# Expert weights of a mixture-of-experts layer loaded in rows of 4 KB, with the down product in parts by whole rows

## The reference

```python
def hier_moe(x, rg, rg_b, re, re_b, wg, wu, wd):     # x: 256 tokens x 1024, 16 experts
    ...                                              # top-1 group of 4, top-2 experts in it
    out = jnp.zeros(t.shape, jnp.float32)
    for e in range(N_EXPERTS):
        h = jax.nn.silu(t @ wg[e]) * (t @ wu[e])     # wg, wu: 1024 x 512, float32
        out = out + combine[:, e:e + 1] * (h @ wd[e])   # wd: 512 x 1024, float32
    return out
...
h = layer_norm(DEEPNORM_ALPHA * h + moe, ln2_g[l], ln2_b[l])
```

## Time and profile before

| | |
|---|---|
| Median of three runs | 524.52 us (523.69 to 528.94) |
| Profiled execution, its span | 522.5 us |
| Between that span and the median | 2.0 us |
| Busy: TensorE matmul, VectorE, ScalarE, GpSimd | 92%, 55%, 28%, 32% of the span |
| The eight expert passes | 275.3 to 509.8 us of the span |

### The profile page before, as it was taken

One profiled execution on the slowest core, in us unless ns is written; L12 is line 12 of the kernel. 1 busy time (PEld: TensorE's weight loads), 2 busy tenths in 40 slices (PEclk: granted clock), 3 DMA queues, 4 the chain that ended last, 5 costly groups with the idle time before them and its releaser, 6 DMA issues.

```text
span 522.5 us, 6332 instructions
## 1 busy us (share of the span) xinstructions
PE 478.6 (92%) x2478; PEld 300.7 (58%) x2478; DVE 287.3 (55%) x497; ACT 148.2 (28%) x223; POOL 165.2 (32%) x94
## 2 busy tenths in 40 slices
PE   7799999997979868769789999999999999999990
PEld 7689998875757756647673434344443434344440
DVE  6069968999999987983552321414031321414136
ACT  3075455554175285322311010101010010101010
POOL 8927707198583909743330000000000000000002
PEclk9999999998999998999999999999999999999996
DMA  7990455545551657459955999999999999999932
GB/s 267 261 355 3 160 182 182 181 161 189 182 174 44 219 211 290 162 170 369 382 205 188 389 386 387 386 387 384 386 387 387 387 387 387 386 387 387 386 133 81
DMA packets 76984, 142.92 MB, mean 274 GB/s; under 512 B 6776, under 2 KB 11009, under 8 KB 76960
## 3 DMA queue, kind: packets, MB, share of 16 engines
q1 hardware_dynamic: 75728, 140.29, 74.8%
q10 hardware_dynamic: 752, 2.11, 1.0%
q0 software_dynamic: 480, 0.20, 0.3%
HBM read 141.54 MB, written 1.05 MB: 273 GB/s over the span
## 4 chain that ended last, share of the span: by engine, by line
PE 61%; DVE 31%; DMA 3%; ACT 2%; issue 2%; SPq 0%; ACTq 0%; DVEq 0%
PE bank L1269 21%; PE bank L1294 11%; DVE ring L1505 7%; PE bank L1235 6%; PE bank L1308 5%; DVE rounded L1426 4%; DVE work L1606 4%; PE bank L1166 4%; PE bank L922 3%; PE bank L951 3%; DMA ring<-in_w_in_dram 3%; DVE ring L1603 2%; DVE ln1p L1463 2%; DVE rounded L1554 2%; PE bank L964 1%
## 5 line engine op out<-in xcount | busy, mean ns | idle before, releaser
L1269 PE MATMUL bank<-ring,gates 128*64 128x512 f32 x512 | 111.6, 594 | 0.4 <-ACT gates L864 0.4
L1040 PE MATMUL bank<-rounded 128*128 128x512 f32 x384 | 94.4, 401 | 6.5 <-POOL rounded L578 4.7
L1040 PEld LDWEIGHTS bank<-rounded 128*128 128x128 f32 x384 | 71.6, 191 | 25.5 <-POOL rounded L578 5.0
L613 POOL TENSOR_TENSOR work<-work,lnp 128x512 f32<-128x512 f32 x1 | 1.3, 1319 | 248.6 <-ACT work L877 248.6
L1269 PEld LDWEIGHTS bank<-ring,gates 128*64 128x64 f32 x512 | 36.2, 137 | 74.3 <-issue 74.3
L1759 DVE TENSOR_TENSOR gates<-gates,bank 128x512 f32<-128x512 f32 x8 | 5.5, 688 | 96.5 <-PE bank L1269 96.5
L1294 PE MATMUL bank<-ring,gates 128*64 128x512 f32 x256 | 58.5, 599 | 0.0
L578 POOL TENSOR_TENSOR rounded<-ring,rounded 128x1024 fp32r<-128x1024 f32 x16 | 39.9, 2524 | 25.1 <-ACT rounded L706 25.1
L586 POOL TENSOR_TENSOR gates<-gates,ring 128x1024 f32<-128x1024 f32 x8 | 34.9, 4360 | 36.0 <-ACT gates L749 36.0
L1235 PEld LDWEIGHTS bank<-gates,work 128*128 128x128 f32 x288 | 34.7, 192 | 13.7 <-issue 13.0
L1235 PE MATMUL bank<-gates,work 128*128 128x128 f32 x288 | 39.3, 281 | 0.7 <-DVE gates L1688 0.7
(11 more groups left out here) (245 smaller groups left out, 618.7 us busy)
## 6 DMA issues: line engine op xcount, KB each, us to landing
ring<-in_expert_w_down_dram SPq DMA_DIRECT2D x32, 1024.0 KB, 14.3
ring<-in_expert_w_up_dram SPq DMA_DIRECT2D x32, 1024.0 KB, 14.2
ring<-in_expert_w_gate_dram SPq DMA_DIRECT2D x32, 1024.0 KB, 14.3
ring<-in_w_in_dram SPq DMA_DIRECT2D x10, 2048.0 KB, 8.5
ring<-in_w_branch_dram SPq DMA_DIRECT2D x2, 2048.0 KB, 8.9
ring<-in_w_out_dram SPq DMA_DIRECT2D x2, 2048.0 KB, 10.7
ring<-in_w_in_dram SPq DMA_DIRECT2D x3, 1024.0 KB, 12.8
ring<-in_b_gate_dram SPq DMA_DIRECT2D x8, 256.0 KB, 4.4
```

The lines of the kernel that those rows point to most:

```text
L1040: last = pe.matmul(bank[:, b, :], hT_part[hpart][:, k, b * P:(b + 1) * P], w[wpart][:, k, :], start=(k == 0 and hpart == wpart), stop=(k = ...
L1269: last = pe.matmul(bank[CAP * e:CAP * e + CAP, part // 2, :], xg[:, FC * h + k, CAP * e:CAP * e + CAP], w[:, e, k, :], start=(h == 0 and k ...
```

## The change

It has three parts.
- **Gate and up matrices.** Two neighbouring rows of the matrix go to one partition: chunk `k` of 128 rows is no longer rows 128`k` to 128`k`+127, but the rows of parity `k` % 2 in block `k` // 2 of 256 rows. A DMA then has rows of 4 KB, which are contiguous over the partitions too. The tokens must have the same order, so `gather` takes every second column of `work` as stationary operand (a step of 8 bytes in place of 4).
- **Down matrices.** They are cut by rows: part 4 holds chunks 0 and 1 with whole rows of 4 KB, part 5 chunks 2 and 3.
- **Order on TensorE.** Each half of the output now needs both parts. The order becomes: down half 0 and half 1 with part 4, down half 0 with part 5, gather chunks 4 and 5, down half 1 with part 5, gather chunks 6 and 7, combine `i` = 0, 1, 2, 3. The release of part 4 has a semaphore of its own, `m_d0`.

VectorE's and ScalarE's code stays as it is.

```diff
-    e_gate = a["expert_w_gate"][0].rearrange("e (k p) f -> p e k f", p=P)
-    e_up = a["expert_w_up"][0].rearrange("e (k p) f -> p e k f", p=P)
+    e_gate = a["expert_w_gate"][0].rearrange("e (j p i) f -> p e j (i f)", p=P, i=2)
+    e_up = a["expert_w_up"][0].rearrange("e (j p i) f -> p e j (i f)", p=P, i=2)
...
-            return ring[:, s, :].rearrange("p (e k n) -> p e k n", e=2, n=HALF)
+            return ring[:, s, :].rearrange("p (e j n) -> p e j n", e=2, n=D)
...
-            e, h = slice(2 * pair, 2 * pair + 2), part % 2
-            if part < 4:
-                return (e_gate, e_up)[part // 2][:, e, h * FC:(h + 1) * FC, :]
-            return e_down[:, e, :, h * HALF:(h + 1) * HALF]
-
-
-        PART_USED = (m_g0, m_g, m_u0, m_u, m_y0, m_y)
+            e, h = slice(2 * pair, 2 * pair + 2), slice(2 * (part % 2), 2 * (part % 2) + 2)
+            return (e_gate, e_up, e_down)[part // 2][:, e, h, :]
+
+
+        PART_USED = (m_g0, m_g, m_u0, m_u, m_d0, m_y)
...
-                                         work[:, t, k * P:(k + 1) * P],
+                                         work[:, t, k // 2 * 2 * P:(k // 2 + 1) * 2 * P]
+                                         .rearrange("p (n i) -> p n i", i=2)[:, :, k % 2],
...
-                                                 xg[:, FC * h + k, CAP * e:CAP * e + CAP], w[:, e, k, :],
+                                                 xg[:, FC * h + k, CAP * e:CAP * e + CAP],
+                                                 w[:, e, k // 2, k % 2 * HALF:(k % 2 + 1) * HALF],
...
-                    for half in range(2):
-                        w = weights(4 + half)
-                        for f in range(FC):
+                    def down(half, part):
+
+                        w = weights(4 + part)
+                        for f in (2 * part, 2 * part + 1):
                             for e in range(2):
                                 last = pe.matmul(bank[CAP * e:CAP * e + CAP, 5 + half, :],
                                                  hexT[:, f * P + CAP * e:f * P + CAP * e + CAP],
-                                                 w[:, e, f, :], start=(f == 0), stop=(f == FC - 1))
-                        last.then_inc(PART_USED[4 + half], 1)
-                        gather(range(4 + 2 * half, 6 + 2 * half))
-                        if half == 0:
-                            pe.wait_ge(m_cTo, it + 1)
-                            pe.wait_ge(m_yd, it + 1)
-                        else:
-                            pe.wait_ge(m_ya, it + 1)
+                                                 w[:, e, f % 2, half * HALF:(half + 1) * HALF],
+                                                 start=(f == 0), stop=(f == FC - 1))
+                        return last
+
+                    def combine(half):
+
                         for t in range(TB):
                             i = 2 * half + t
                             if i >= 2:
...
+                    down(0, 0)
+                    down(1, 0).then_inc(m_d0, 1)
+                    down(0, 1).then_inc(m_y0, 1)
+                    gather(range(4, 6))
+                    down(1, 1).then_inc(m_y, 1)
+                    gather(range(6, 8))
+                    pe.wait_ge(m_cTo, it + 1)
+                    pe.wait_ge(m_yd, it + 1)
+                    combine(0)
+                    pe.wait_ge(m_ya, it + 1)
+                    combine(1)
```

More of the change, by code:

```diff
@@ L321, in hybrid_trunk_kernel @@
         m_cTo = sem("combine_turned_out")
+        m_d0 = sem("expert_down_first_chunks_used")
         m_y0 = sem("expert_output_first_half_in_psum")
```

## The result

The changed kernel takes 534.59 us (median of four runs, 533.83 to 537.04) against 526.18 for the kernel before (the three runs given above and a fourth, 523.69 to 528.94). The medians are 8.4 us apart, which is 1.6%. The ratio on record, an estimate from all these runs, is 1.0182, with a 95% interval of 1.0148 to 1.0215, that is 7.8 to 11.3 us. The profiled executions differ by 10.0 us: their spans are 532.5 and 522.5 us.

What follows compares the result with a forecast made beforehand. TensorE was taken to bound the passes, with the loads close behind. The new wait's 5.3 us and the last pass's 1.6, with 0 for loads, gather and reordering, added 6.9 to 524.5: 531.4 us, range 527.0 to 536.0.

Steps and rivals of the forecast that it cites:

- What bounds: Expert passes: TensorE is busy for the whole 29.30 us; the last loads come 1.6 and 3.3 us early.
- Slower rows: Rival on the load stream: the new rows run slower, at 369 GB/s costing 2.8 us more, 534.2; chance 0.05.
- late loads: Rival: loads late before, repaired by the change, at most 2.0 us back, 529.4; chance 0.13 together with hidden refills.
- The rate that the prediction quoted: Load stream: 408.7 GB/s listed for rows of 4 KiB, 5.6% faster than 387, last parts some 10 us earlier.
- The new wait: Combine `i` = 2 and 3 wait for VectorE's additions to free their banks: 0.76 us a pass, 5.3 in seven.
- Its inner steps: Combine matmuls: `i` = 2 starts at 1.73, `i` = 3 at 3.15, 0.05 us behind VectorE, each with a 0.21 us refill.
- the 0.35 to 0.6 that were to show it: Sign: idle TensorE in us at the second half's combine matmuls, ended by VectorE's addition, seven or eight times.
- The forecast for the last pass: Last pass, which VectorE ends: the gathered chunks' copy now follows the second statistics, fourth addition ends later; 1.6 us.
- The reordered product and the gathers: Down product in blocks of 24 and 8 records, with gathers and combines: 12.81 us against 12.85, taken as 0.
- Gather with a step: Gather's stationary operand with a step of 8 bytes: 0 taken, upper end 31.7 us; slow-load rival has chance 0.08.
- The rule of 16-byte lines: Gather's reads: full bandwidth while at least two hit the same 16-byte line, so a step of 8 bytes costs 0.
- The sum: Whole kernel: 5.3 + 1.6 + 0 + 0 = 6.9 us, giving 531.4 us; forecast of 5 to 8.5 us has chance 0.71.

Runs made afterwards that it cites:

- the merged order on the old loads: Kernel before, its loads and gather kept, with the whole down product in one block, then gather and combine in turns: 525.84 us, ratio 1.0003.
- the down parts alone: Changed kernel with the old gate and up loads and old gather, so down matrices by whole rows and the new order: 531.92 us, ratio 1.0133.
- Moving the statistics: Changed kernel with VectorE's two statistics of the half row moved behind both additions: 530.13 us, ratio 1.0081.
- putting the combine back: Changed kernel with combine `i` = 0 and 1 put back ahead of the last quarter of the down product: 527.11 us, ratio 1.0033.
- the kernel with the 16-byte step: Changed kernel with combine `i` = 0 and 1 put back, and gate and up rows of 8 KB: 560.94 us, ratio 1.0647 to the kernel before.

## Why the prediction was right

- **What bounds.** TensorE, with the loads 1.6 us behind it: held. Slower rows and late loads (rivals) did not come; the stream gained 5.7% and TensorE none of it. The rate that the prediction quoted from the Trainium skill (page "DMA: Bandwidth & Descriptors", section "iDMA fabric — 4 AXI ports for 8 engines, asymmetric across TPBs"), 408.7 GB/s for rows of 4 KiB, is what the trace shows, 409. That the small slack was real is shown by the merged order on the old loads.
- **The new wait: 0.76 us a pass.** Measured 0.78 with the down parts alone, and 7.0 us in the whole against 6.9. Moving the statistics took 0.56 of it away, putting the combine back took away all of it. Its inner steps held too: `i` = 3 started 0.06 us behind the second addition and took 1.12 in place of 0.87 us. The idle time in TensorE's matmul rows is 0.29 us a pass, a little under the 0.35 to 0.6 that were to show it; the rest is refill. The forecast for the last pass was 1.6 us; measured were 1.7, of which 0.16 are the gather's.
- **The reordered product and the gathers: 0.** The blocks of 24 and 8 records took 5.30 and 1.87 us, forecast were 5.31 and 1.87. (Four combine matmuls at 0.87 are 3.48 us and not the 3.45 of the prediction's sum, which changes nothing in the result.)
- **Gather with a step: 0 taken, of 0 to 31.7 us.** Measured 0.16 us a pass, 1.3 us in eight. It was mis-sized by this much: a load takes 4 ns longer (196 in place of 192), and as nothing covers a gather's loads, each group shows it. The rule of 16-byte lines that the prediction quoted from the Trainium skill ("SBUF — State Buffer", section "Door 1: The DMA port swizzle (why `[64,N]` ≈ `[32,N]`)") is borne out in direction by the two steps: with two values to a line a load takes 4 ns more, with one value 137 ns more. The upper end of 110 ns a load, worked out from rows for a step of 8 bytes, is of the size that a step of 16 bytes then cost.
- **The sum: 6.9 us.** Measured in the passes 8.5, of which the gather's 1.3 were not in it: without them 7.2. The medians are 8.4 us apart, so they agree with the passes. The profile shows 10.0, with 1.5 us ahead of the passes. Since 1.3 of these 1.5 arose before any expert load and lie inside the spread of that start over all profiles, I put them down to that spread; the runs do not prove it for this pair of executions. The time forecast was 531.4 us, and 534.59 was measured, inside the range of 527 to 536 but near its end. Of these 3.2 us, 1.7 are the kernel before itself, whose median rose from 524.52 to 526.18 with the fourth run, and 1.3 the gather's.

## What to carry to other kernels

Before loads are made faster, read how early they land: here 1.6 us early meant that a stream 5.7% faster was worth nothing, and with half of the gate and up products left out it was worth 8 us. A reordering that the new layout seems to demand must be costed by what stood between two uses of the same bank; the data layout wanted whole rows, but not that the four combine matmuls stand together. The step in the stationary operand cost 4 ns a load at two float32 values to 16 bytes, and at one value it doubled a gather group.

## What was not expected of the hardware

- The stepped stationary operand: 192, 196 and 329 ns a load for steps of 4, 8 and 16 bytes, so the price jumps between the last two. With 16 bytes a gather group doubled from 0.94 to 1.87 us.
- The part ahead of the passes ends at 274.9 to 280.3 us in twelve profiles, the kernel with the 16-byte step left aside. A single profile's span is then no measure for changes of 1% here; the pass lengths are.
